# The last body of the up projections as block pairs, and the down projections with two outputs by turns and another order of k tiles

## What is computed

```python
def swiglu(x, w_in, w_out):                 # D_MODEL 1024, D_FF 2816, SEQ 512
    g, u = jnp.split(x @ w_in, 2, axis=-1)
    return (jax.nn.silu(g) * u) @ w_out
# first block, four times:  h = h + 0.5 * swiglu(rms_norm(h, g), w_in, w_out)
# second block, once:       h = h + swiglu_2(rmsnorm(h, g), w_gate_up, w_down)
```

## Time and profile before

| what | value |
|---|---|
| median of three runs | 2781.37 us (2779.88 to 2786.25) |
| the profiled execution | 2780.14 us, its span 2778.3 us |
| PE busy | 2752.1 us, 99% of the span |
| POOL, DVE, ACT busy | 1573.6, 1657.7, 1329.5 us |
| chain that ended last | PE 94%, DVE 3%, ACT 1%, issue 1% |
| DMA | 96 GB/s mean |

### The profile page before, as it was taken

The page is one execution under the profiler, slowest core; times in us unless marked ns, Lnnn a source line. Parts: engine busy times, 40 slices in busy tenths (PEclk is TensorE's granted clock), DMA queues, the critical chain, the costliest instruction groups (busy, mean ns, idle before and its releaser), DMA issues.

```text
span 2778.3 us, 45558 instructions
## 1 busy us (share of the span) xinstructions
PE 2752.1 (99%) x16386; PEld 2353.0 (85%) x16386; DVE 1657.7 (60%) x2703; ACT 1329.5 (48%) x2076; POOL 1573.6 (57%) x872
## 2 busy tenths in 40 slices
PE   8999999999999999999999999999999999999999
PEld 6998877899889998888999886665688888799987
DVE  6776147677616774135777316589789464467730
ACT  5554267555425553244555333566444444455531
POOL 5775445677547784444777443158633373277843
PEclk9999999999999999999999999999999999999999
DMA  3334322233322333332233331112222342123332
GB/s 138 106 111 118 98 84 84 92 107 120 105 93 92 118 114 99 100 107 84 96 116 126 92 111 61 54 46 69 77 84 73 102 152 76 54 92 115 117 99 77
DMA packets 80685, 267.91 MB, mean 96 GB/s; under 512 B 11168, under 2 KB 13216, under 8 KB 80560
## 3 DMA queue, kind: packets, MB, share of 16 engines
q1 hardware_dynamic: 77904, 262.01, 28.4%
q10 hardware_dynamic: 2656, 4.26, 0.5%
HBM read 263.09 MB, written 2.10 MB: 95 GB/s over the span
## 4 chain that ended last, share of the span: by engine, by line
PE 94%; DVE 3%; ACT 1%; issue 1%; DMA 0%; POOL 0%; ACTq 0%; SPq 0%; DVEq 0%
PE bank L467 18%; PE bank L468 17%; PE bank L469 17%; PE bank L725 10%; PE bank L723 10%; PE bank L724 10%; PE bank L554 1%; PE bank L556 1%; PE bank L555 1%; PE bank L1660 1%; PE bank L2072 1%; PE bank L2940 1%; PE bank L2672 0%; PE bank L2081 0%; PE bank L2652 0%
## 5 line engine op out<-in xcount | busy, mean ns | idle before, releaser
L455 POOL TENSOR_TENSOR ring_lo<-w_stage,ring_hi 128x1024 fp32r<-128x1024 f32 (+1 forms) x228 | 535.9, 2356 | 712.9 <-ACT ring_hi L431 712.7
L431 ACT ACTIVATE ring_hi<-w_stage 128x1024 fp32r<-128x1024 f32 (+1 forms) x324 | 328.6, 1020 | 358.0 <-PE bank L469 297.1
L820 POOL TENSOR_TENSOR ring_lo<-w_stage,ring_hi 128x1024 fp32r<-128x1024 f32 (+1 forms) x176 | 325.8, 1851 | 146.6 <-ACT ring_hi L929 146.3
L467 PE MATMUL bank<-xg_hi,ring_hi 128*128 128x512 f32 x976 | 396.2, 406 | 4.6 <-DVE h_raw L1088 3.4
L468 PE MATMUL bank<-xg_lo,ring_hi 128*128 128x512 f32 x976 | 381.3, 391 | 0.0
L469 PE MATMUL bank<-xg_hi,ring_lo 128*128 128x512 f32 x976 | 381.0, 390 | 0.0
L462 POOL TENSOR_TENSOR ring_lo<-w_stage,ring_hi 128x1024 fp32r<-128x1024 f32 (+1 forms) x96 | 234.7, 2450 | 257.0 <-ACT ring_hi L431 212.6
L467 PE MATMUL bank<-h_hi,ring_hi 128*128 128x512 f32 x880 | 342.3, 389 | 0.0
L468 PE MATMUL bank<-h_lo,ring_hi 128*128 128x512 f32 x880 | 342.3, 389 | 0.0
L469 PE MATMUL bank<-h_hi,ring_lo 128*128 128x512 f32 x880 | 342.3, 389 | 0.0
L723 PE MATMUL bank<-xsum,s_w 128*128 128x256 f32 x1056 | 291.7, 276 | 0.0
(11 more groups left out here) (531 smaller groups left out, 6679.3 us busy)
## 6 DMA issues: line engine op xcount, KB each, us to landing
w_stage<-w_up SPq DMA_DIRECT2D x220, 512.0 KB, 4.2
w_stage<-w_down SPq DMA_DIRECT2D x80, 512.0 KB, 3.5
w_stage<-merge SPq DMA_DIRECT2D x36, 512.0 KB, 3.4
w_stage<-w_down SPq DMA_DIRECT2D x40, 384.0 KB, 3.1
w_stage<-hg_qfg SPq DMA_DIRECT2D x12, 512.0 KB, 3.4
w_stage<-rec_r SPq DMA_DIRECT2D x8, 512.0 KB, 3.5
w_stage<-rec_y SPq DMA_DIRECT2D x8, 512.0 KB, 3.4
w_stage<-rec_out SPq DMA_DIRECT2D x8, 512.0 KB, 3.4
```

What stands on the lines that cost most here:

```text
L431: act.activation(w_hi[:, r, 0:w], w_stage[:, r, 0:w], ACT.Copy).then_inc(w_hi_ready, 1)
L455: pool.tensor_tensor(w_lo[:, r, 0:w], w_stage[:, r, 0:w], f32(w_hi[:, r, 0:w]), ALU.subtract).then_inc(w_lo_ready, 1)
L467: pe.matmul(out, w_hi[:, r, c], hi, start=start, stop=False)
L820: pool.tensor_tensor(wb_lo[:, r, cs], w_stage[:, r, cs], f32(wb_hi[:, r, cs]), ALU.subtract).then_inc(w_lo_ready, 1)
```

## The change

The last body of each up projection is computed as two block pairs too (`PAIRS` goes from KF - 4 to KF - 2, 98 in all). In the down projections, the first two outputs of a body are taken by turns (k tile by k tile, m = 0 then m = 1), the other two one after the other; units are ordered by `DOWN_UNITS`, k tiles by `DOWN_K`, and the weights' rows are laid out in that order. ACT's and DVE's `high` and `low` follow `DOWN_K`; ACT waits for M5, M7 and M6 of the last block pair ahead of groups of them. POOL's splits of the down units stand written out behind the up projection's steps. Loads of the down units have a function of their own, `load_down`.

```diff
+DOWN_UNITS = ((0, 0), (1, 0), (0, 1), (1, 1), (0, 2), (1, 2), (2, 0), (2, 1), (2, 2), (3, 0), (3, 1), (3, 2))
+DOWN_K = (12, 13, 14, 15, 0, 1, 2, 3, 16, 17, 8, 9, 10, 11, 4, 5, 6, 7, 18, 19, 20, 21)
+    def load_down(sp, L, i):
+        for b in range(L.bodies):
+            for u, w in enumerate(L.widths):
+                if b == 0 and u < RING:
+                    sp.wait_ge(w_lo_ready, L.base + (u | 1) + 1 - RING)
+                    sp.wait_ge(wsum_done, after_wsum(i, "S4", pair_at(LAST, u // 2)))
+                else:
+                    sp.wait_ge(w_lo_ready, L.base + b * L.per + u + 1 - RING)
+                sp.dma_start(w_stage[:, u % RING, 0:w], L.src(b, u)).then_inc(w_loaded[u % RING], 16)
-    PAIRS = KF - 4
+    PAIRS = KF - 2
@@ pe_ffn
-        with pe.Fori(PLAIN_FIRST[i] + 1, LAST) as b:
+        with pe.Fori(PLAIN_FIRST[i] + 1, LAST + 1) as b:
             step(b, 0)
             step(b, 1)
-        plain(LAST)
         def down(b):
-            for m in range(4):
-                pe.wait_ge(taken, b * 4 + (L.rbase + (m | 1) + 1 - RING))
+            for outs in ((0, 1), (2,), (3,)):
+                for m in outs:
+                    pe.wait_ge(taken, b * 4 + (L.rbase + (m | 1) + 1 - RING))
                 for part in range(3):
...
+                    for at in range(8 * part, min(8 * part + 8, KF)):
+                        k = DOWN_K[at]
+                        for m in outs:
+                            u = DOWN_UNITS.index((m, part))
+                            if at == 8 * part:
+                                pe.wait_ge(w_lo_ready, b * L.per + (L.base + u + 1))
+                            if m == 0:
+                                pe.wait_ge(h_lo_ready, KF * i + at + 1)
+                            mm = three_passes(pe, bank[m][:], u % RING, at - 8 * part, h_hi[:, k, :], h_lo[:, k, :],
+                                              at == 0, at == KF - 1)
@@ pool_up
-        with pool.Fori(at + 1, LAST - 1) as b:
+        with pool.Fori(at + 1, LAST) as b:
             step(b, 0)
             step(b, 1)
-        step(LAST - 1, 0)
-        plain(LAST, 0)
-        scale_gate(KF - 4)
-        plain(LAST, 1)
-        plain(LAST, 2)
-        scale_gate(KF - 3)
-        plain(LAST, 3)
+        step(LAST, 0)
+        L = layers[f"down{i}"]
+        split_lo_unit(pool, L, 0, 0)
+        scale_gate(KF - 2)
+        split_lo_unit(pool, L, 0, 1)
+        split_lo_unit(pool, L, 0, 2)
+        scale_gate(KF - 1)
+        for u in range(3, L.n):
+            split_lo_unit(pool, L, u // L.per, u % L.per)
@@ act_ffn
-        step(LAST - 1, 0)
+        step(LAST, 0)
+        split_hi(act, L, 0, 0)
         copy_m1(PAIRS - 1, 1)
-        split_hi(act, U, LAST, 0)
-        split_hi(act, U, LAST, 1)
-        silu(KF - 4)
...
         split_hi(act, L, 0, 1)
         silu(KF - 2)
-        for j in range(12, 18):
-            high(j)
+        act.wait_ge(block_mm, after_block(i, "M5", PAIRS - 1))
+        for k in range(4):
+            high(k)
         split_hi(act, L, 0, 2)
-        for j in range(18, 21):
-            high(j)
+        for k in range(4, 10):
+            high(k)
+        act.wait_ge(block_mm, after_block(i, "M7", PAIRS - 1))
+        for k in range(10, 14):
+            high(k)
+        act.wait_ge(block_mm, after_block(i, "M6", PAIRS - 1))
         silu(KF - 1)
-        high(KF - 1)
+        for k in range(14, KF):
+            high(k)
@@ dve_ffn
-        step(LAST - 1, 0)
+        step(LAST, 0)
         u2_sum(PAIRS - 2, 0)
         other_sums(PAIRS - 2, 0)
...
+        take_gate(KF - 2, 0)
+        product(KF - 2, 0)
+        for k in range(6):
+            low(k)
         u2_sum(PAIRS - 1, 1)
         other_sums(PAIRS - 1, 1)
...
         take_gate(KF - 1, 1)
-        low(20)
+        for k in range(6, 16):
+            low(k)
         product(KF - 1, 1)
-        low(21)
+        for k in range(16, KF):
+            low(k)
@@ layout
-        out[f"w_down{i}"] = columns(down)
+        out[f"w_down{i}"] = columns(down.reshape(KF, P, D)[list(DOWN_K)].reshape(KF * P, D))
```

More of the change, by code:

```diff
@@ L109, in layer @@
         layers[name] = order[-1]
-    DOWN_W = [UNIT, UNIT, KF * P - 2 * UNIT]
     def ffn_layers(i):
         layer(f"up{i}", f"w_up{i}", [UNIT] * 4, 11, 44)
-        layer(f"down{i}", f"w_down{i}", DOWN_W * 4, 2, 8,
-              cols=lambda j: (j // 3, (j % 3) * UNIT, min((j % 3 + 1) * UNIT, KF * P)))
+        layer(f"down{i}", f"w_down{i}", [min(UNIT, KF * P - part * UNIT) for _, part in DOWN_UNITS], 2, 8,
+              cols=lambda j: (DOWN_UNITS[j][0], DOWN_UNITS[j][1] * UNIT, min((DOWN_UNITS[j][1] + 1) * UNIT, KF * P)))
     def column_layer(name, n, widths=(UNIT,) * 4, results=None):
@@ L642, in build @@
     PLAIN_FIRST = (2, 1, 1, 1, 1)
-    PAIRS = KF - 4
+    PAIRS = KF - 2
     LAST = KF // 2 - 1
     FFN_OF = {f"up{i}": i for i in range(5)}
+    DOWN_OF = {f"down{i}": i for i in range(5)}
     XSUM_COUNT = {0: 4, 1: 8, 2: 9, 3: 13}
@@ L788, in pe_ffn @@
         step(PLAIN_FIRST[i], 1)
-        with pe.Fori(PLAIN_FIRST[i] + 1, LAST) as b:
+        with pe.Fori(PLAIN_FIRST[i] + 1, LAST + 1) as b:
             step(b, 0)
             step(b, 1)
-        plain(LAST)
         def down(b):
-            for m in range(4):
-                pe.wait_ge(taken, b * 4 + (L.rbase + (m | 1) + 1 - RING))
+            for outs in ((0, 1), (2,), (3,)):
+                for m in outs:
+                    pe.wait_ge(taken, b * 4 + (L.rbase + (m | 1) + 1 - RING))
                 for part in range(3):
[L798 to L806, removed]
+                    for at in range(8 * part, min(8 * part + 8, KF)):
[8 more added lines that the diff above has]
+                                              at == 0, at == KF - 1)
+                            if at == min(8 * part + 8, KF) - 1:
+                                mm.then_inc(unit_used, 1)
         each_body(pe, L.bodies, down)
@@ L962, in silu, with high @@
             act.activation(gbuf[:], gbuf[:], ACT.Silu).then_inc(silu_done, 1)
-        def high(j):
+        def high(at):
+            j = DOWN_K[at]
             act.wait_ge(taken, j * 2 + (U.rbase + 2))
@@ L1005, in act_ffn @@
         step(at, 1)
-        with act.Fori(at + 1, LAST - 1) as b:
+        with act.Fori(at + 1, LAST) as b:
             step(b, 0)
             step(b, 1)
-        step(LAST - 1, 0)
+        step(LAST, 0)
+        split_hi(act, L, 0, 0)
         copy_m1(PAIRS - 1, 1)
-        split_hi(act, U, LAST, 0)
-        split_hi(act, U, LAST, 1)
-        silu(KF - 4)
[L1014 to L1017, removed]
-            high(j)
-        split_hi(act, L, 0, 0)
-        for j in range(6, 12):
-            high(j)
         split_hi(act, L, 0, 1)
         silu(KF - 2)
-        for j in range(12, 18):
-            high(j)
+        act.wait_ge(block_mm, after_block(i, "M5", PAIRS - 1))
+        for k in range(4):
+            high(k)
         split_hi(act, L, 0, 2)
-        for j in range(18, 21):
-            high(j)
+        for k in range(4, 10):
[4 more added lines that the diff above has]
+        act.wait_ge(block_mm, after_block(i, "M6", PAIRS - 1))
         silu(KF - 1)
-        high(KF - 1)
+        for k in range(14, KF):
+            high(k)
     def dve_ffn(dve, i, gain=None):
@@ L1072, in is_plain @@
         def is_plain(j):
-            return isinstance(j, int) and (j < 2 * PLAIN_FIRST[i] or j >= KF - 2)
+            return isinstance(j, int) and j < 2 * PLAIN_FIRST[i]
         def take_gate(j, p):
@@ L1088, in product, with low @@
             dve.tensor_tensor(tile(h_raw, j), gbuf[:], u_bank(p)[:], ALU.mult).then_inc(taken, 1)
-        def low(j):
-            dve.wait_ge(h_hi_ready, KF * i + j + 1)
+        def low(at):
+            j = DOWN_K[at]
+            dve.wait_ge(h_hi_ready, KF * i + at + 1)
             dve.tensor_tensor(h_lo[:, j, :], h_raw[:, j, :], f32(h_hi[:, j, :]), ALU.subtract).then_inc(h_lo_ready, 1)
@@ L1124, in dve_ffn, with done_unit, done_at @@
         step(at, 1)
-        with dve.Fori(at + 1, LAST - 1) as b:
+        with dve.Fori(at + 1, LAST) as b:
             step(b, 0)
             step(b, 1)
-        step(LAST - 1, 0)
+        step(LAST, 0)
         u2_sum(PAIRS - 2, 0)
         other_sums(PAIRS - 2, 0)
-        take_gate(KF - 4, 0)
-        product(KF - 4, 0)
+        take_gate(KF - 2, 0)
+        product(KF - 2, 0)
+        for k in range(6):
+            low(k)
         u2_sum(PAIRS - 1, 1)
         other_sums(PAIRS - 1, 1)
[L1135 to L1144, removed]
         take_gate(KF - 1, 1)
-        low(20)
+        for k in range(6, 16):
+            low(k)
         product(KF - 1, 1)
-        low(21)
+        for k in range(16, KF):
+            low(k)
+    def done_unit(L, mm):
+        return DOWN_UNITS.index((mm, 2)) if L.name in DOWN_OF else mm
+    def done_at(L, i):
+        if L.name in DOWN_OF:
+            return DOWN_UNITS[i][0] if DOWN_UNITS[i][1] == 2 else None
+        return i
```

(18 more changed lines are left out.)

2 lines of the change are left out of this document (added).

## The result

The changed kernel took 2830.3 us (median of 4 runs, 2830.03 to 2833.8) against 2780.8 for the kernel before on the same chip: ratio 1.018, 95% interval 1.0167 to 1.0192. It is slower by 1.8%, where 2827 (1.6%) was forecast with a range of 2808 to 2842.

What follows compares the result with a forecast made beforehand. PE, busy 99% of the span, was taken as the bound: -13.75 (block pairs) + 42 (unit 3 waits) + 7.5 (FFN 1 and 3) + 10 (clock) = +45.8, so 2827 us, range 2808 to 2842.

Steps and rivals of the forecast that it cites:

- ten block pairs: Last up-projection body: two plain pairs in each of 5 FFNs become block pairs, each saving 1.375 us, 13.75 in all.
- waits for unit 3, FFN 0, 2, 4: Down projection: PE stands from +11.6 to +20.0 for the late split of unit 3, 8.4 us in each FFN.
- the same, FFN 1 and 3: The 8.4 us wait, plus 3.2 (S5 coefficients, FFN 1) and 4.3 (final gain, FFN 3), together 7.5 more.
- clock: After each long wait PE runs matmuls at half clock: 2.0 us lost each, 10 in all, ends 0 and 3.2.
- Steps of the chain in FFN 4: Up-to-down transition: forecast times of ACT, POOL and DVE steps, leading to unit 3 being ready at +20.0.
- E: The moment at which PE ends the last block pair of an up projection; the forecast counts its times from it.
- the split itself: POOL's split of down unit 3, behind the last product: forecast to take 2.4 us.
- E + 11.6: Down projection: when PE wants unit 3, after 51 matmuls of 0.227 us.
- the row's 1.6: FFN 0, profile before: after a 3.44 us wait eight matmuls took 0.425 in place of 0.227, 1.6 us lost.
- the cover holds: Rival: unit 3 is ready by +11.6 in each FFN, PE has no gap, 2767.6 us; chance 6%.
- Short waits: Rival: low halves run as if POOL were not there, waits 3.5 us each, 2793 to 2801 us; chance 9%.
- Long waits: Rival: one more low half caught and the split stretched to 2.86; waits 11 us each, 2848 us; chance 8%.

Runs made afterwards that it cites:

- experiment 3: Changed kernel with down units 3 and 2 split at other places and ACT's final-gain wait moved to the gain's first read: 2770.2 us, ratio 0.996.
- Experiment 7: Changed kernel, but in FFN 0, 2 and 4 DVE holds its last six low halves until POOL has split down unit 3: 2827.2 us, ratio 1.0161.
- experiment 8: Changed kernel with DVE's last product eight low halves earlier (behind low(7), not low(15)), unit 3 still behind it: 2814.6 us, ratio 1.0111.
- experiment 5: Changed kernel with unit 3 split earlier and the down projection's outputs one after the other again: 2805.3 us, ratio 1.008.
- experiment 4: Changed kernel with the down projection's outputs one after the other again, unit 3 still late: 2804.7 us, ratio 1.0083.
- experiment 6: Kernel before with the turns alone, k tiles in old order and last up body plain: 2789.9 us, ratio 1.0032.

## Why the prediction was right

The terms of its sum, each with what it measured in the profiled execution of after:

| term | forecast | measured |
|---|---|---|
| ten block pairs | -13.75 | -13.75 by the pitch; 11 net in experiment 3 |
| waits for unit 3, FFN 0, 2, 4 | 25.2 | 29.1 (9.69 each, 1.1 of it at `low(1)`) |
| the same, FFN 1 and 3 | 16.8 + 7.5 | 23.4 (11.08 and 12.33) |
| clock | 10 | 9.8 (49 slow matmuls, 0.2 each) |
| pieces of 0.1 to 0.4 us behind the waits | 0 | 3.0 |
| sum | +45.8 | +51.5 |

The span grew by 53.7; of the other 2.2 us about 1.6 lie ahead of FFN 0's down projection, where the wait at 41 us is. The median grew by 49.5, which is 3.7 above the forecast. By two terms the sum is too low: the waits (+3.9 in FFN 0, 2 and 4, -0.9 in FFN 1 and 3) and the pieces, for which it had nothing (0.36 at the first matmul behind a long wait, 0.1 behind `low(1)` and at the last slow matmul). What was forecast for PE's busy time was off too: 14 less the slow matmuls' 10 would be a fall of some 4 us, and it fell by 0.3; the pieces account for most of that.

Steps of the chain in FFN 4, from E: product of pair 20 ended at -2.6 (forecast -2.6), `low(0)` at -0.4 (-0.35), the gate of the last pair at +7.8 (+8.0), POOL's scaling at +10.2 (+10.5), the last product at +15.6 (+15.9), POOL's split began at +17.2 (+17.6). Up to here nothing is off by more than 0.4 us. **The mis-sized term is the split itself**: 4.12 us in the place of 2.4, so unit 3 was ready at +21.4 and not +20.0. The low half beside a split had shown only one side of the two engines' quarrel, DVE waiting for POOL. Here DVE ended four low halves in a row, 0.60 us apart, after POOL's split had begun, and the split ended 2.2 us after the last of them, about the time that it takes alone. Experiment 7 shows that these low halves are what held it up.

That PE's wait for unit 3 is 8.42 us in the profile, where 8.4 was forecast, is luck: the wait for `low(1)` made PE come to unit 3 some 1.2 us later than E + 11.6, and the longer split moved the wait's end by 1.4. From +11.6 on PE lost 9.7 and not 8.4.

The same error hid the second one: FFN 1 and 3 were to wait 3.2 and 4.3 longer than the others, and did so by 1.4 and 2.6 only. The later start was right (in FFN 1 the coefficients come first), but by then DVE had finished its low halves and the split took 2.35; 3.2 less the 1.8 saved is 1.4, and 4.3 less 1.8 is 2.5.

The clock's 2.0 us for each wait, more than the row's 1.6 and less than twice that, was right on average: 8 to 12 slow matmuls behind a wait. It was a choice between two values and not worked out, and in experiment 8 waits of equal length (3.14 to 3.18) were followed by 0, 13 and 7 slow matmuls, so its closeness is partly luck. That an idle array falls to half rate and has to be busy for a while before it gets full rate back is what the Trainium skill (TensorE: Matmul & The Clock Gate, Part 1) says; the trace agrees for these five waits of 8.4 to 11.05 us.

The rivals: "the cover holds" fell, but its figure, 2767.6, is within 3 us of what the kernel does once unit 3, unit 2 and the wait for the final gain are all moved (experiment 3); with unit 3 alone it is 2775.1. "Short waits" needed DVE and POOL not to meet; they do. "Long waits" had one of its two causes right, the split made longer by low halves beside it, but at 2.86 us, and it took 4.12; its other cause, one more low half held up, did not occur.

## What to carry to other kernels

When a change brings a consumer forward, list everything that it will ask for and look for each item's place in its producer's queue, not only for how long the producer needs: here 1 us of ACT and 2.4 of POOL were free all the time, and cost 55 us because they stood behind an instruction that had become the last of a long chain. A run-ahead constant (AHEAD = 3) hides such a place, as the instruction isn't written where the others are. And a wait for a value belongs where it is read: `final_gain` stood ahead of splits that don't need it.

## What the hardware showed that was not expected

- POOL and DVE, both with SBUF operands, hold each other up, and either can lose. A DVE low half (0.60 us alone) took up to 2.94 beside splits (experiment 3); a split (2.4 alone) took 4.12 and 4.64 beside a row of low halves, and 2.37 in the same kernel as the 4.64, in another FFN. The Trainium skill (GPSIMD Engine Reference, Key points) names the contention; these are its sizes here.
- Which of the two goes first went, in all ten traces, with the moment at which the split begins. There are 28 splits of 128x1024 that began while DVE was in a low half that had not itself been held up, with another low half behind it. Of these 18 began 0.37 to 0.52 us after that low half's start: POOL went at once (2.37 to 2.57 us), and the next low half took 2.50 to 2.88. The other ten began 0.56 to 0.57 us after it (nine) or 0.06 after it (one): DVE's row went on at 0.60, and the split took 4.12 to 4.64. These are only a few different moments, repeated from FFN to FFN, and why they decide isn't shown. Between the two groups lie 0.04 us in the start of the split and at least 1.5 us in its length.
- PE's granted clock fell to 0.50 also after three waits of 1.06, 2.62 and 0.74 us within 9 us (experiment 5, FFN 4), but not after those of experiment 4 in FFN 0 and 4, which are alike in number and length. In experiment 6 one wait of 2.18 us (FFN 3) was followed by seven slow matmuls and one of 3.16 (FFN 1) by none. The length of a wait alone doesn't tell what the clock will do.
- A wait costs PE more than the idle time that the profile gives: 0.94 us of idle before `low(1)` moved the next start by 1.10 and the one after by 0.1 more. In a row of matmuls the next one starts 0.227 us after the last, while that one still has 0.16 of the 0.39 us to go that the profile gives it; behind a wait this overlap is lost, which is the 0.16.
